# A hybrid decoder step on one core: the input is also read turned, and the token scales are spread by a small transpose

## The reference

```python
def rmsnorm(x, w):
    xf = x.astype(jnp.float32)
    y = xf * lax.rsqrt(jnp.mean(xf * xf, axis=-1, keepdims=True) + EPS)
    return (y * w.astype(jnp.float32)).astype(x.dtype)
...
xn = rmsnorm(x, p["attn_norm_w"])
proj = xn @ p["w_in"]
q, k, v, mq, mk, mv, mo, mi, mf, ga, gb = jnp.split(proj, points, axis=-1)
```

## Time and profile before

| | us |
|---|---|
| median of 3 runs | 1459.51 (1459.5 to 1461.03) |
| the profiled execution, its own time | 1460.65 |
| its span, first to last instruction | 1458.9 |
| TensorE busy (PE) | 1412.6 |
| VectorE busy (DVE) | 1021.4 |
| ScalarE busy (ACT) | 695.7 |
| mean granted clock of TensorE | 0.988 |

### The profile page before, as it was taken

One profiled execution on the slowest core, in us unless ns is written; L12 is line 12 of the kernel. 1 busy time (PEld: TensorE's weight loads), 2 busy tenths in 40 slices (PEclk: granted clock), 3 DMA queues, 4 the chain that ended last, 5 costly groups with the idle time before them and its releaser, 6 DMA issues.

```text
span 1458.9 us, 21697 instructions
## 1 busy us (share of the span) xinstructions
PE 1412.6 (97%) x8070; PEld 1264.6 (87%) x8070; DVE 1021.4 (70%) x1390; ACT 695.7 (48%) x831; POOL 455.3 (31%) x368
## 2 busy tenths in 40 slices
PE   7999999999999999899999989999999999999996
PEld 6899999999999999889888777888888888888885
DVE  4522321147666667767766689999999999999995
ACT  6421121145444445332312127777777777776662
POOL 2600000011111110100100045547775555555464
PEclk9999999999999999999999979999999999999999
DMA  6335669534333332757772279999999999999972
GB/s 205 123 136 199 221 227 51 107 114 125 111 109 106 106 104 72 212 184 229 238 295 115 109 250 399 366 421 417 403 415 393 403 393 401 397 395 405 388 312 70
DMA packets 164907, 354.81 MB, mean 243 GB/s; under 512 B 39214, under 2 KB 117490, under 8 KB 139152
## 3 DMA queue, kind: packets, MB, share of 16 engines
q1 hardware_dynamic: 137752, 324.97, 62.5%
q0 software_dynamic: 26560, 28.82, 5.8%
q10 hardware_dynamic: 536, 0.26, 0.1%
HBM read 319.53 MB, written 101.54 MB: 289 GB/s over the span
## 4 chain that ended last, share of the span: by engine, by line
PE 47%; DVE 3%; ACT 0%; issue 0%; POOLq 0%; POOL 0%; DVEq 0%; ACTq 0%
PE xt_ey L2832 4%; PE xt_ey L2834 4%; PE xt_ey L2833 4%; PE y_h_up L2811 4%; PE y_h_up L2812 4%; PE y_h_up L2810 4%; PE logits_gate L2810 2%; PE logits_gate L2812 2%; PE logits_gate L2811 2%; PE ranks_gate L2810 2%; PE y_x L2797 2%; PE ranks_gate L2811 2%; PE ranks_gate L2812 2%; PE y_x L2212 1%; PE y_h_up L2818 1%; PE y_h_up L2212 1%
## 5 line engine op out<-in xcount | busy, mean ns | idle before, releaser
L2670 DVE TENSOR_TENSOR e_w_lo<-w_out,e_w_hi 128x2048 fp32r<-128x2048 f32 x64 | 143.6, 2283 | 0.0
L2670 DVE TENSOR_TENSOR e_w_lo<-mixed,e_w_hi 128x2048 fp32r<-128x2048 f32 x62 | 140.6, 2287 | 2.8 <-ACT e_w_hi L2606 2.0
L1019 PE MATMUL gate_banks<-f_hi,wg_hi 128*128 128x368 f32 (+1 forms) x376 | 126.6, 337 | 1.0 <-PEq L187 0.5
L2606 ACT CAST e_w_hi<-w_out 128x2048 fp32r<-128x2048 f32 x64 | 123.0, 1921 | 1.7 <-PE y_h_up L2812 0.8
L1021 PE MATMUL gate_banks<-f_hi,wg_lo 128*128 128x368 f32 (+1 forms) x376 | 123.3, 328 | 0.0
L1020 PE MATMUL gate_banks<-f_lo,wg_hi 128*128 128x368 f32 (+1 forms) x376 | 123.2, 328 | 0.0
L2606 ACT CAST e_w_hi<-mixed 128x2048 fp32r<-128x2048 f32 x62 | 115.5, 1915 | 2.5 <-PE logits_gate L2812 2.5
L2832 PE MATMUL xt_ey<-e_w_hi,e_hT_hi 128*128 128x512 f32 x256 | 102.6, 401 | 1.9 <-DVE e_w_lo L2670 1.6
L2810 PE MATMUL y_h_up<-e_w_hi,e_x_hi 128*128 128x512 f32 x256 | 99.7, 390 | 0.8 <-DVE e_w_lo L2670 0.8
L2834 PE MATMUL xt_ey<-e_w_hi,e_hT_lo 128*128 128x512 f32 x256 | 100.0, 391 | 0.0
L2833 PE MATMUL xt_ey<-e_w_lo,e_hT_hi 128*128 128x512 f32 x256 | 99.9, 390 | 0.0
(11 more groups left out here) (671 smaller groups left out, 3980.3 us busy)
## 6 DMA issues: line engine op xcount, KB each, us to landing
w_out<-in_w_down_e SPq DMA_DIRECT2D x64, 1024.0 KB, 7.2
mixed<-in_w_gate_e SPq DMA_DIRECT2D x32, 1024.0 KB, 7.4
mixed<-in_w_up_e SPq DMA_DIRECT2D x32, 1024.0 KB, 7.2
w_gate<-in_w_gate_e SPq DMA_DIRECT2D x32, 1024.0 KB, 7.4
w_up<-in_w_up_e SPq DMA_DIRECT2D x32, 1024.0 KB, 7.2
group_rows<-zeros SPq DMA_DIRECT2D x8, 2048.0 KB, 12.7
proj<-mixed SPq DMA_DIRECT2D x8, 1408.0 KB, 5.4
w_ring<-in_w_in SPq DMA_DIRECT2D x7, 1408.0 KB, 17.3
```

Of the source, the lines that this page charges most:

```text
L1019: pe.matmul(bank, wg_hi[j][:, k, :], hi, start=(k == 0), stop=False)
L2606: act.copy(hi(i, step, j), raw(i, u, j)).then_inc(hi_ready[i], 1)
L2670: dve.tensor_tensor(lo(i, u, j), raw(i, u, j), hi(i, step, j).bitcast(F32), ALU.subtract).then_inc(lo_ready[i], 1)
```

## The change

x comes a second time as an input that the host lays out turned, `x_T` (features by tokens). SP loads from it, behind each `x_tile[t]`, the tile's 128 columns (8 x 128 pieces of 512 bytes) into `x_turned`, which lies where `f_lo` is written later. `square(t)` waits for both loads. `scale(t)` and the eight transposes of `turn_x(t)` go. In their place `spread_scale(t)` on TensorE transposes `rstd` of the tile, broadcast along the free axis: one 128x128 transpose, which puts the scale of token j into column j of every partition of bank 6 or 7. `turned(t)` on VectorE then does eight scalar_tensor_tensor of 128 columns: turned x, times the norm weight of the feature (a scalar for each partition), times the scales in PSUM.

The lists are ordered anew as well: ScalarE does `square(1)` behind the two weight casts; VectorE does `turned(t)` ahead of `feat_lo(t-1)`; the norm weights and the first weights are loaded behind tile 0; POOL's memset of `gates` no longer waits for the last transpose.

```diff
@@ -153,13 +153,15 @@
         banks = [S["gate_banks"][:, 512 * b:512 * b + 512] for b in range(3)]
         banks += [ctx.enter_context(nc.psum_tensor(f"pj{b}", [P, 512], F32)) for b in range(3, 8)]
         x_loaded = [sem(f"x_loaded{t}") for t in range(NT + 1)]
+        x_turned = nc.alloc_sbuf_tensor_at("x_turned", [P, KD, T], F32, offset=S["f_lo_at"])
+        x_turned_view = a["x_T"].rearrange("(k p) t -> p k t", p=P)
         norm_w_loaded, small_loaded = sem("norm_w_loaded"), sem("small_loaded")
-        ssq_ready, rstd_ready, xn_ready = sem("ssq_ready"), sem("rstd_ready"), sem("xn_ready")
+        ssq_ready, rstd_ready = sem("ssq_ready"), sem("rstd_ready")
         ms_ready, constants_ready = sem("ms_ready"), sem("constants_ready")
         zeros_ready, spare_filled = sem("zeros_ready"), sem("spare_filled")
         featT_ready, f_hi_ready, f_lo_ready = sem("featT_ready"), sem("f_hi_ready"), sem("f_lo_ready")
         w_hi_ready, w_lo_ready = ([sem(f"w_{n}_ready{v}") for v in range(2)] for n in ("hi", "lo"))
-        xt_full, xt_free = [sem(f"xt_full{h}") for h in range(2)], [sem(f"xt_free{h}") for h in range(2)]
+        scale_full, scale_free = [sem(f"scale_full{u}") for u in range(2)], [sem(f"scale_free{u}") for u in range(2)]
         w_loaded = [sem(f"w_loaded{v}") for v in range(2)]
         first_half_loaded = sem("first_half_loaded")
         full = [sem(f"pj_full{b}") for b in range(6)]
@@ -235,9 +237,10 @@
                     sp.dma_start(a["proj"][TP:T, columns(n, CW)], stage[v][:TS, NT, :]).then_inc(stored[v], 16)
 
                 for t in range(NT + 1):
-                    src = xs if t == NT else a["x_prompt"][0, t * P:(t + 1) * P, :]
+                    src, cols = xs if t == NT else a["x_prompt"][0, t * P:(t + 1) * P, :], slice(t * P, t * P + tile_rows(t))
                     sp.dma_start(x_tile[t][:tile_rows(t)], src).then_inc(x_loaded[t], 16)
-                    if t == 1:
+                    sp.dma_start(x_turned[:, :, cols], x_turned_view[:, :, cols]).then_inc(x_loaded[t], 16)
+                    if t == 0:
                         sp.dma_start(S["attn_nw"][:], a["attn_norm_w"][0].rearrange("(k p) -> p k", p=P)).then_inc(norm_w_loaded, 16)
                         for i, ks in enumerate(FIRST_HALVES):
                             sp.dma_start(w_ring[0][:, ks, 0:width[0]], w_view[:, ks, columns(0, width[0])]).then_inc(w_loaded[0] if i else first_half_loaded, 16)
@@ -290,14 +293,9 @@
             def _(act):
                 def square(t):
                     r = tile_rows(t)
-                    act.wait_ge(x_loaded[t], 16)
+                    act.wait_ge(x_loaded[t], 32)
                     act.activation(junk[:r], x_tile[t][:r], ACT.Square, scale=float(D) ** -0.5, accum_out=ssq[:r, t:t + 1]).then_inc(ssq_ready, 1)
                     act.wait_ge(ssq_ready, t + 1)
-
-                def scale(t):
-                    r = tile_rows(t)
-                    act.wait_ge(rstd_ready, t + 1)
-                    act.activation(x_tile[t][:r], x_tile[t][:r], ACT.Copy, scale=rstd[:r, t:t + 1]).then_inc(xn_ready, 1)
 
                 def feat_hi(t, r):
                     act.wait_ge(featT_ready, t + 1)
@@ -341,16 +339,13 @@
                     act.activation(wprev[:], wprev[:], ACT.Exp).then_inc(rows_exp, 1)
 
                 square(0)
-                square(1)
-                scale(0)
-                scale(1)
                 first_split_hi(0)
                 feat_hi(0, P)
                 first_split_hi(1)
+                square(1)
                 for t in range(2, NT + 1):
                     square(t)
                     feat_hi(t - 1, P)
-                    scale(t)
                     if t >= 4 and t % 2 == 0:
                         evacuate(act, 0, act.copy, 0, only=t - 4)
                     if t == 7:
@@ -391,13 +386,12 @@
                 pool.memset(nobody[:, 0:WEIGHT], SKIP)
                 pool.memset(zeros[:], 0.0).then_inc(zeros_ready, 1)
                 constants(pool, S, dist, constants_ready)
-                pool.wait_ge(xt_full[1], NT + 1)
                 pool.memset(gates[:], 0.0).then_inc(ms_ready, 1)
 
             @block.vector
             def _(dve):
                 for h in range(2):
-                    dve.sem_inc(xt_free[h], 1)
+                    dve.sem_inc(scale_free[h], 1)
                 for b in range(6):
                     dve.sem_inc(free[b], 1)
                 dve.wait_ge(norm_w_loaded, 16)
@@ -405,14 +399,13 @@
                 def turned(t, r):
                     if t >= 2:
                         dve.wait_ge(f_lo_ready, t - 1)
-                    for h in range(2):
-                        dve.wait_ge(xt_full[h], t + 1)
-                        w = S["attn_nw"][:, 4 * h:4 * h + 4]
-                        ins = dve.tensor_tensor(f_tile[t % 2][:, 4 * h:4 * h + 4, 0:r],
-                                                banks[6 + h][:, :].rearrange("p (k t) -> p k t", k=4)[:, :, :r],
-                                                bc(w, 2, r), ALU.mult)
-                        ins.then_inc(xt_free[h], 1)
-                    dve.wait_ge(xt_free[1], t + 2)
+                    dve.wait_ge(x_loaded[t], 32)
+                    dve.wait_ge(scale_full[t % 2], t // 2 + 1)
+                    for k in range(KD):
+                        ins = dve.scalar_tensor_tensor(f_tile[t % 2][:, k, 0:r], feat(x_turned, t, r)[:, k, :], S["attn_nw"][:, k:k + 1],
+                                                       banks[6 + t % 2][:, 0:r], ALU.mult, ALU.mult)
+                    ins.then_inc(scale_free[t % 2], 1)
+                    dve.wait_ge(scale_free[t % 2], t // 2 + 2)
                     dve.sem_inc(featT_ready, 1)
 
                 def feat_lo(t, r):
@@ -498,10 +491,11 @@
                 feat_lo(0, P)
                 first_split_lo(1)
                 turned(1, P)
-                feat_lo(1, P)
                 for t in range(2, NT + 1):
                     turned(t, tile_rows(t))
-                    feat_lo(t, tile_rows(t))
+                    feat_lo(t - 1, P)
+                    if t == NT:
+                        feat_lo(t, TS)
                     if t in (4, 6):
                         evacuate(dve, 1, dve.tensor_copy, 0, only=t - 3)
                     if t == 7:
@@ -554,22 +548,18 @@
                         ins = pe.matmul(banks[b][:r, :w], lo, w_hi[v][:, k, 0:w], start=False, stop=(k == KD - 1))
                     ins.then_inc(full[b], 1)
 
-                def turn_x(t):
+                def spread_scale(t):
                     r = tile_rows(t)
-                    pe.wait_ge(xn_ready, t + 1)
-                    for h in range(2):
-                        pe.wait_ge(xt_free[h], t + 1)
-                        for k in range(4):
-                            c = (4 * h + k) * P
-                            ins = pe.transpose(banks[6 + h][:, k * P:k * P + r], x_tile[t][:r, c:c + P], S["ident"][:r, :r])
-                        ins.then_inc(xt_full[h], 1)
-
-                turn_x(0)
-                turn_x(1)
+                    pe.wait_ge(rstd_ready, t + 1)
+                    pe.wait_ge(scale_free[t % 2], t // 2 + 1)
+                    pe.transpose(banks[6 + t % 2][:, 0:r], rstd[:r, t:t + 1].broadcast_to([r, P]), S["ident"][:r, :r]).then_inc(scale_full[t % 2], 1)
+
+                spread_scale(0)
+                spread_scale(1)
                 for t in range(NT - 1):
                     pe.wait_ge(f_lo_ready, t + 1)
                     product(0, 0, t, width[0], t == 0)
-                    turn_x(t + 2)
+                    spread_scale(t + 2)
                 for t in range(NT - 1, NT + 1):
                     pe.wait_ge(f_lo_ready, t + 1)
                     product(0, 0, t, width[0])
@@ -3036,6 +3026,8 @@
     for name in INS:
         arrays["in_" + name] = np.ascontiguousarray(inputs[name])
         a[name] = nc.dram_tensor("in_" + name, arrays["in_" + name].shape, F32, kind="ExternalInput").ap()
+    arrays["in_x_T"] = np.ascontiguousarray(np.concatenate([inputs["x_prompt"][0], np.reshape(inputs["x_sample"], (TS, D))]).T)
+    a["x_T"] = nc.dram_tensor("in_x_T", (D, T), F32, kind="ExternalInput").ap()
     for name, shape in OUTS:
         a[name] = nc.dram_tensor(name, shape, F32, kind="ExternalOutput").ap()
     for name, shape in SCRATCH:
```

## The result

The changed kernel takes 1497.44 us (median of 4; 1493.96 to 1498.89) against 1460.27 (median of 4) for the kernel before: a ratio of 1.0235, with a 95% interval of 1.0209 to 1.0261. (Ratios and intervals here are those on record; the quotient of two medians can differ a little, here it is 1.0255.) It is slower, and inside the predicted range of 1477 to 1502. The predicted time was 1488.1, that is +28.6 on 1459.5; measured is +37.2. That is above the forecast's own range of 1482 to 1494. The mechanism was there, one of its sizes was too small.

What follows compares the result with a forecast made beforehand. TensorE, busy for 97% of the span, was taken as the bound. Terms +1.9 + 21.5 + 9.5 - 3.0 - 1.3 = +28.6 on 1459.5 gave 1488.1 us; own range 1482 to 1494, 8-in-10 range 1477 to 1502.

Steps and rivals of the forecast that it cites:

- start of product 0: Stage start: tile 0's square waits for its turned load, square(1) follows the casts; product 0 at about 16.0, +1.9 us.
- product 0 itself: First product, 5.59 us before: left as it was, with up to 1.7 us more kept for the range.
- seven gaps: TensorE between products 0 to 7: 3.94 us each instead of 0.79, the seventh 0.5 less; +21.5 us.
- clock in products 1 to 7: Part of each product runs at the lower clock after idle gaps: 1.35 us each, +9.5 us.
- last stall: TensorE's wait of 3.0 us before product 8 goes, since ScalarE's side casts come due when product 7 starts: -3.0 us.
- product 8 at full pace: Product 8 no longer runs at a slow clock behind a stall: -1.3 us.
- The closed chain: First stage: end of product t, transpose, eight VectorE multiplies, feat_lo(t+1), product t+1, nothing beside a product; 3.94 us a link.
- rival B: Clock low for whole products 1 to 7: 13 us more, +41.6, 1501.1 us; chance 0.12.
- Rival A: Clock stays up through the gaps, the 9.5 us falls away: +19.1, 1478.6 us; chance 0.13.
- D: Loads bound the first stage, a tile's 1.05 MB taking 12.6 us: 23 us more, +52, 1511 us; chance 0.04.
- C: Faster: VectorE has its scale 3.5 us before product t ends, gaps of 0.1 us: -7.2, 1452.3 us; chance 0.03.
- the second load of x: Extra turned loads in the first stage: costed at nothing, each tile's 1.05 MB given 8 to 9 us by the chain.

Runs made afterwards that it cites:

- The order alone: Kernel before, with only VectorE's turned(t) moved ahead of feat_lo(t-1), no turned loads or small multiplies: 1484.7 us, ratio 1.0134.
- undoing the order: Changed kernel with VectorE's old order, turned(t) then feat_lo(t), and the scale still transposed behind the product: 1465.7 us, ratio 1.0033.
- one-multiply run: Changed kernel without the features' norm weights in the first stage, one multiply of 1024 columns replacing the eight: 1481.5 us, ratio 1.0136.
- the filled gaps: Changed kernel plus 20 matmuls of 360 columns, with unused results, behind each spread scale: 1482.4 us, ratio 1.0129.
- loads-alone run: Kernel before plus the turned loads, which nothing reads, square(t) waiting for them, weights issued behind tile 0: 1468.4 us, ratio 1.0041.
- the best version: Changed kernel, scale transposed at the head of products 1 to 6, chunk 1's weight cast and subtraction moved behind tile 8: 1456.4 us, ratio 0.9955.
- the late split: Chunk 1's weight cast and subtraction moved from tile 7's place to behind tile 8; in the kernel before, 1459.5 us, ratio 0.9976.
- The scale at the head alone: Changed kernel, tile t+2's scale transposed at the head of product t for t = 1 to 5, mid-product for 0 and 6: 1459.7 us, ratio 0.9992.
- the two runs with the square earlier: Square of tile 1 moved ahead of the second weight cast: with scale at the product's head 1459.3 us (0.998), in the changed kernel 1499.0 (1.0254).
- scale in mid-product: Changed kernel, transpose of tile t+2's scale moved from behind product t to after 12 of its 24 matmuls: 1472.5 us, ratio 1.0061.

## Why the prediction was right, and where it was short

The forecast's signs came: seven waits of TensorE for `f_lo`, 3.7 each, the eight multiplies behind each product's end, product 8 directly behind product 7. Only the end of the stage was at 96 and not at 89. Term by term, from the starts in the profile (us):

| step | predicted | measured |
|---|---|---|
| start of product 0 | +1.9 | +2.1 (16.20) |
| product 0 itself | 0 | +0.7 (6.27) |
| seven gaps | +21.5 | +22.1 (4.00 each, 3.46) |
| clock in products 1 to 7 | +9.5 | +15.3 (43.8 against 28.5) |
| last stall | -3.0 | -3.0 |
| product 8 at full pace | -1.3 | -1.3 |
| end of stage | +28.6 | +35.9 |
| behind the stage | 0 | +1.3 |

- The closed chain was read from the order of the calls, and was right. The order alone brings most of the loss into the kernel before, and undoing the order, or moving the transpose to the head of the product, takes it out.
- The eight multiplies were priced at 2.17 by a row of the same shape and took 2.15 to 2.16. The prediction worked out 1.55 from the table of the Trainium skill ("VectorE: DVE Perf Modes", section on the TRN2 errata) with its figure for sources in SBUF, 58 cycles. These multiplies also read PSUM, and with the table's figure for that, 120 cycles, the estimate is 8 x (120 + 128) / 0.96 GHz = 2.07, which the trace agrees with within 0.1. The advice of the Trainium skill there, few large operations instead of many small, the one-multiply run bears out: 1.22 against 2.16.
- The clock's term was mis-sized: 5.8 of the 8.6 us that the forecast was short. I took 1.35 for each product from two stalls of 2 to 3 us. Behind gaps of 4.0 the products lost 1.6 to 2.6, 2.2 on average. The forecast and rival B (3.2 each) had bracketed it. That it is the clock, the filled gaps show. The time was inside the stated range only because that range reached to B: 1497.4 is nearer to B's 1501.1 than to the forecast's 1488.1.
- Product 0 was left at its old length, and took 0.7 more; the prediction had kept up to 1.7 of it for the range.
- The last stall went as forecast. Its source was VectorE's list more than ScalarE's casts: in the kernel before the subtraction of chunk 1 (3.28) stands ahead of `turned(8)`, and moving it away alone ends the stall.
- Rival A (the clock stays up) is refuted by a granted clock of 0.71. D (the loads) is refuted by the loads-alone run in the steady part. B's whole products at the low level did not come: between 12 and 19 of 24 matmuls were slow. C, the faster end, exists but needs the scale at the head of the product; its price of -7.2 was near what the best version reached together with the late split (0.9955, -6.6), about half of which the late split gives by itself. The scale at the head alone stood at 0.9992, not told apart from no change: C had left out the split of chunk 1, which stands in VectorE's list.
- Costed at nothing, the second load of x: right for the steady part. At the start it depends on the order on ScalarE: 7.5 us in the old order. In the changed kernel nothing came beyond the +1.9 forecast but 0.2, yet the load is not free there: in the two runs with the square earlier, tile 1's load held it until 12.9 and 13.4, about where it stands now (13.17) behind the casts.

## What to carry to other kernels

When a software pipeline is made one step deeper on one engine, each producer that it waits for has to move one step earlier too, or the wait closes a ring with the work it was to run beside; follow each wait in each list from the consumer back to the consumer. A chain of length c that is released from within a block of length b hides only behind what is left of the block, so it must be released at the head if c is near b. And price a gap of TensorE with its clock: here 22 us of gaps brought 15 us of slower matmuls.

## What the runs showed of the hardware that was not expected

How many products lost clock rose with the time that TensorE was idle in gaps that return every tile. In the profiled executions (one of each kernel) the products 1 to 7 that lost over 1 us to the clock were:

| run | idle before most products | slow products |
|---|---|---|
| scale in mid-product | 1.8 | 1 of 7 |
| order alone (the gap of 3.4 holds eight transposes) | 2.4 | 3 of 7 |
| one multiply | 2.8 | 4 of 7 |
| changed kernel, and square of tile 1 earlier | 3.7 | 7 of 7 in both |

In the changed kernel they were also slow for longer: 12 to 19 matmuls of 24 at half pace, against 9 to 12 behind the single stalls of the kernel before. Twenty matmuls in each gap of 4.0, whose results nobody reads, gave back 15 us of 37. The Trainium skill ("TensorE: Matmul & The Clock Gate", section on HAM oscillation) tells of a matmul loop with a wait in each tile that lost its clock in every tile; the changed kernel agrees with it, at a granted clock of 0.71, and the runs with shorter idle times only in part.

GpSimd's small operations took longer beside VectorE's long subtractions: 3.28 instead of 0.54 beside one of 3.08 us, and at the start of the changed kernel 1.00 (14.39 to 15.39) instead of 0.19 beside one of 1.65, which delays the scale of tile 1 and so product 0. Turned loads of 1024 pieces of 512 bytes each ran beside the rest without a wait in the steady part.
